# The next expert's rows, transposed one part later, in a mixture-of-experts decoder step

## The chip, the core and the metric

The kernel runs on one core of a Trainium2 chip. The metric is the device time of one execution in microseconds (us). The core has TensorE (PE in the rows, PEld for its weight loads), the vector engine (DVE), the scalar engine (ACT), GpSimd (POOL) and SyncE (SP), which here only issues DMAs. They run apart from one another and meet by semaphores.

## What is computed

One decoder layer for 512 prompt tokens and 32 sample tokens: attention, a short convolution and memory attention, then a mixture of experts, and a last RMSNorm. Each of the 544 tokens goes to 4 of 32 experts. Everything is float32. What matters here is the part for the experts:

```python
h = xb @ w_gate_up[e] + b_gate_up[e]
gate = jnp.minimum(h[:, 0::2], SWIGLU_LIMIT)
up = jnp.clip(h[:, 1::2], -SWIGLU_LIMIT, SWIGLU_LIMIT)
glu = gate * jax.nn.sigmoid(gate * SWIGLU_ALPHA)
return ((up + 1.0) * glu) @ w_down[e] + b_down[e]
```

`xb` are the rows of the tokens that chose expert `e`, with 1024 columns; `w_gate_up[e]` is 1024 x 2048 and `w_down[e]` 1024 x 1024. The results are scaled by the gates and added to the tokens' rows.

## The kernel before

**Stages.** From 0 to some 245 us the kernel does attention, the router and the tables that say which token sits in which slot of which expert. Then come 32 periods, one for each expert. Each expert has 104 slots; a block for overflow stands behind and isn't entered with these inputs.

**Precision.** Each float32 operand is split into a high part (rounded to the fast matmul type, by a cast on ACT) and a low part (the rest, by a subtraction on DVE). A product is then three matmuls: high x high, low x high, high x low (lines 2435, 2436, 2437), each 104 x 512 over 128 rows.

**Parts.** The weights of an expert come as six chunks of 2 MB, each used as two halves. A half is a part: twelve matmuls on TensorE, one cast on ACT (`high_part`, line 1133) and one subtraction on DVE (`low_part`, line 1754). The twelve parts of period `n` are, in TensorE's order: gate-up parts 0 to 5 of expert n, down parts 6 and 7 of expert n, gate-up parts 8 and 9 that already belong to expert n+1, and down parts 10 and 11 of expert n. Between them stand the transposes of the expert's activations: `act_rows`, four transposes each, behind part 4 and behind part 8 (line 2430). Each part ends with one increment of the semaphore `w_used`, which releases buffers for the other engines: after part i of period n it stands at 12n + 3 + i.

**The next expert's rows.** GpSimd gathers them from DRAM two periods ahead (`gather`, line 749; in the loop, from the ninth expert on, behind two small copies of slot tables, lines 740 and 741). TensorE transposes them (`x_rows`, line 2419, eight transposes into two PSUM banks), ACT casts them (`x_high`, line 1164, twice), and DVE subtracts (`x_low`, line 1818, twice). Gate-up part 8 is the first to read them. The first matmul of part 8 also waits for the bias row that ACT copies into its PSUM bank (`bias_seed`, line 1171) and for its weights' low half.

**Order on ACT at the place in question** (i is the part): in step 6 the clamp of the gate (line 1149), `x_high`, the sigmoid (line 1155), the cast of weight part 9 (line 1133), the copy of the first bias row (line 1171). **On DVE** in step 6: the clip (line 1829), `x_low`, the subtraction of weight part 8, and the two products of the SwiGLU (lines 1836 and 1839). The order is written out by hand, in one program per engine. Period 1 alone is written otherwise, by the flag `late`: there the transposes stand behind down part 6, and `x_high` and `x_low` behind the sigmoid and the SwiGLU.

**On GpSimd** in a period: the scatter of the last expert's results into the token table (line 762), two broadcasts of a bias row (line 682), then the wait for `w_used` at 12n + 9 (behind part 6). Behind that wait: in periods 1 to 3 the add of one tile of bias rows (line 814), and in all that still gather, the gather and two more broadcasts. Periods 2 to 6 end with four writes of the slot table (line 733).

Of the kernel before, what the change touches and what calls it, by code (L numbers as in the profile page):

```python
# [55 lines left out]
HALVES = 2 * NCH  # L56
# [56 lines left out]
def build(nc, x_prompt, x_sample, mem_prompt, cache_win_k, cache_win_v, win_kT, mem_kT, cache_mem_v,  # L113
# [4 lines left out]
    with ctx:  # L118
# [13 lines left out]
        def sem(name):  # L132
            if name not in sems:
                sems[name] = ctx.enter_context(nc.semaphore(name))
            return sems[name]
# [34 lines left out]
        def c_(name, rows=P):  # L170
            a, b = _C[name]
            return cst[0:rows, a:b]
# [172 lines left out]
        def row_tile(r):  # L345
            return (memrow[:, r, :], P) if r < 2 else (xrow[0:ROWS[r - 2], r - 2, :], ROWS[r - 2])
# [293 lines left out]
        def _(pool):  # L640
# [6 lines left out]
            for r in range(7):  # L647
                n = row_tile(r)[1]
# [130 lines left out]
            def period(n, k, last=False, table=False, bare=False, overflow=False):  # L779
                old = not (last or table or bare)  # L780
                if old:
                    slots(n + 2, k)
                if not isinstance(n, int) or n > 0:
                    scatter(n, k)
                if not last:
                    if overflow:
                        bias_rows(n + 1, 0)
                    bias_rows(n + 1, 1)
                    pool.wait_ge(sem("w_used"), n * HALVES + 9)
                if isinstance(n, int) and 0 < n < UB:  # L790
                    pool.wait_ge(sem("scattered"), n * 16)
                    add_bias(n + 1)
                if table:
                    table_slots(n + 2, k + 2)
                if old or table:
                    gather(n + 2, k + 2, table)
                if old and not overflow or table:
                    bias_rows(n + 2, 0)
                if old and isinstance(n, int) and 2 <= n < 7:
                    table_rows(4 * (n - 2), 4 * (n - 1))  # L800
# [67 lines left out]
        def _(ac):  # L868
# [3 lines left out]
            for r in range(7):  # L872
                ap, n = row_tile(r)
# [339 lines left out]
            def period(n, k, last=False):  # L1213
                for i in range(10 if last else HALVES):
                    if i == 0 and (not isinstance(n, int) or n > 0):
                        y_rows(n, k, n * HALVES + 2)
                    if i == 2:
                        gate_over(n, 0)
                        gate_sigmoid(n, 0)
                    if i == 6:  # L1220
                        late = isinstance(n, int) and n == 1
                        gate_over(n, 1)
                        if not last and not late:
                            x_high(n + 1)
                        gate_sigmoid(n, 1)
                        if late:
                            x_high(n + 1)
                    if not last or i + 3 < 10:
                        high_part(n, i + 3, last)
                    if isinstance(n, int) and n < UB and (i == 1 or i == 0 == n):  # L1230
                        bias_evict(n + i)
                    if last and i == 5:
                        row_squares(2, 1)
                    if last and i == 6:
                        row_squares(3, 1)
                        row_squares(4, 1)
                    if last and i == 7:
                        act_high(n, 1)
                        row_squares(0, 1)
                        row_squares(1, 1)  # L1240
                    if i == 4:
                        act_high(n, 0)
                    if i == 6 and not last:
                        bias_seed(n + 1, 0)
                    if i == 8 and not last:
                        act_high(n, 1)
                    if i >= 9 and not last:
                        bias_seed(n + 1, i - 8)
# [10 lines left out]
            for c, part in enumerate((2, 3, 2)):  # L1259
                last = nc.scalar.copy(gate3[:, :, c * NE:(c + 1) * NE], rv_all[:, 0:NE, :, part].rearrange("p e j -> p j e"))  # L1260
# [15 lines left out]
            for u in range(2 * UB):  # L1276
                period(u, u)
# [27 lines left out]
        def _(dv):  # L1305
# [296 lines left out]
            for j in range(NTT):  # L1602
                last = v.tensor_scalar(row_i[:, j:j + 1], c_("tokid")[:, j:j + 1], float(NT), None, ALU.add)
# [299 lines left out]
            def period(n, k, last=False, table=False, bare=False):  # L1903
                old = not (last or table or bare)
                for i in range(10 if last else HALVES):
                    if i == 2:
                        clip_up(n, 0)
                    if i == 6:
                        late = isinstance(n, int) and n == 1
                        clip_up(n, 1)  # L1910
                        if not last and not late:
                            x_low(n + 1)
                    if i == (7 if last else 9):
                        act_low(n, 1)
                    if last and i == 7:
                        row_means(3, 1)
                        row_means(4, 1)
                    if i == 10 and old:
                        slot_info(n + 2, k + 2)
                    if not last or i + 2 < 10:  # L1920
                        low_part(n, i + 2, last)
                    if i == 0 and old:
                        hot_slots(n + 2, k)
                    if isinstance(n, int) and n == 0 and i == 4:
                        table_keys()
                    if isinstance(n, int) and n == 0 and i == 8:
                        table_tops()
                    if isinstance(n, int) and n == 1 and i in (1, 4, 7, 10):
                        table_gates(i // 3)
                    if i == 2:  # L1930
                        swiglu(n, 0)
                    if i == 4:
                        act_low(n, 0)
                    if i == 6:
                        swiglu(n, 1)
                        if late:
                            x_low(n + 1)
                    if last and i == 6:
                        row_means(2, 1)
                        row_weights(0, 1)  # L1940
                        row_weights(1, 1)
# [29 lines left out]
        def _(pe):  # L1971
# [366 lines left out]
            for c in range(2):  # L2338
                last = tr(banks[7][0:18, 256 + c * P:256 + (c + 1) * P], ul[:, c, :], ident)
# [156 lines left out]
            def period(n, k, last=False, table=False, bare=False, overflow=False):  # L2496

                early = n if isinstance(n, int) and n < UB else None
                if early == 0:
                    bias_term(0)  # L2500
                if early is not None:
                    pe.wait_ge(sem("gcol_ready"), early + 2)
                    bias_term(early + 1)
                gate_up(n, 0, last, k)
                gate_up(n, 1, last, k)
                gate_up(n, 2, last, k)
                gate_up(n, 3, last, k)
                if early is not None:
                    pe.wait_ge(sem("bias_row"), 2 * early + 4)
                gate_up(n, 4, last, k)  # L2510
                act_rows(n, 0, overflow)
                gate_up(n, 5, last, k)
                late = isinstance(n, int) and n == 1
                if not last and not late:
                    x_rows(n + 1, k + 1)
                wait(pe, "yrow_ready", n * 2)
                down(n, 6, last)
                if late:
                    x_rows(n + 1, k + 1)
                down(n, 7, last, middle=last)  # L2520
                if not last:
                    pe.wait_ge(sem("x_low"), n * 2 + 4)
                    gate_up(n, 8, last, k + 1)
                    act_rows(n, 1)
                    gate_up(n, 9, last, k + 1)
                    if not (table or bare):
                        info(n + 2, k)
                down(n, 8 if last else 10, last)
                down(n, 9 if last else 11, last)
# [3 lines left out]
            for j in range(NTT):  # L2533
                last = mm(banks[6][0:CAP, 416:418], hot[:, 0, j, :], rv_all[:, 0, j, 0:2], start=(j == 0), stop=(j == NTT - 1))
# [4 lines left out]
            for j in range(NTT):  # L2539
                last = mm(banks[6][0:CAP, 416:420], hot[:, 0, j, :], rv_all[:, 0, j, :], start=(j == 0), stop=(j == NTT - 1))  # L2540
# [4 lines left out]
            for q in range(4):  # L2545
                last = mm(banks[q][0:CAP, :], bias_r[:, 0:CAP], bias_r[:, 0:512], start=True, stop=True)
# [67 lines left out]
```

## Time and profile before

| what | value |
|---|---|
| median of 3 runs | 1394.35 us (1400.48, 1394.35, 1393.88) |
| profiled execution | 1399.39 us, of which the span is 1397.5 |
| mean granted clock of TensorE | 0.989 of full speed |
| busy: TensorE, DVE, ACT, GpSimd | 1359.8, 1206.0, 1070.6, 759.1 us |
| moved by DMA | 461.48 MB, 330 GB/s in the mean |

The span runs from the first to the last instruction; the profiled execution's own time is 1.9 us longer. Busy time is the time in which an engine has an instruction in hand; for TensorE the ends of matmuls are modelled and overlap, so the distance between two starts tells more than the duration of one. A timeline row gives the start, the duration, the engine, the line, the operation, what it writes and reads, a count of merged instructions, and in brackets the idle time just before it and what ended that. Where several semaphores are waited for, the one named is the one that the profile found last; a DMA can be the true one. A row by stage gives the stretch, its length, and busy time with the count of instructions for PE, PEld, DVE, ACT and POOL.

### The profile page before, as it was taken

To read this page: it belongs to the slowest core of one execution; us is meant where nothing else is said; L and a number is where in the kernel's file an instruction comes from. 1 tells how busy PE (TensorE), PEld (TensorE's weight loads), DVE (VectorE), ACT (ScalarE), POOL (GpSimd) and SP (SyncE) were. 2 spreads that over 40 slices of the span, in tenths; PEclk is the share of its full clock that TensorE was granted. 3 is DMA by queue.
4 is the path that set the end of the run, shared out by engine and by line. 5 is a ranking of instruction groups with operands and counts; after the bars stand their busy time and mean duration, and the time that the engine had idled before them with its cause. 6 is when DMAs were issued, how large, how long until landed. Compare 5 with 4: busy or idle time off the path is not lost.

```text
span 1397.5 us, 19410 instructions
## 1 busy us (share of the span) xinstructions
PE 1359.8 (97%) x6775; PEld 1000.4 (72%) x6775; DVE 1206.0 (86%) x1098; ACT 1070.6 (77%) x1102; POOL 759.1 (54%) x363
## 2 busy tenths in 40 slices
PE   9999998999997999999999999999999999999995
PEld 6988655667775777777777777777777777777773
DVE  5466555899996999999999999999999999999996
ACT  5354413878885888888888888888888888888884
POOL 2022112386775979656666666566665666665403
PEclk9999999999998999999999999999999999999998
DMA  9522171999997999999999999999999999999984
GB/s 353 196 66 83 75 286 61 367 378 372 388 391 269 363 386 364 366 387 382 381 390 388 369 385 369 382 384 376 383 381 370 383 376 378 391 376 377 383 304 149
DMA packets 52506, 461.48 MB, mean 330 GB/s; under 512 B 11545, under 2 KB 15611, under 8 KB 26825
## 3 DMA queue, kind: packets, MB, share of 16 engines
q1 hardware_dynamic: 40169, 438.59, 80.2%
q0 software_dynamic: 10624, 20.42, 6.5%
q10 hardware_dynamic: 1648, 1.65, 0.4%
q8 instruction: 36, 0.59, 0.2%
q14 instruction: 29, 0.24, 0.0%
HBM read 446.88 MB, written 24.31 MB: 337 GB/s over the span
## 4 chain that ended last, share of the span: by engine, by line
PE 67%; DMA 2%; issue 1%; POOL 1%; DVE 0%; ACT 0%; POOLq 0%; ACTq 0%; DVEq 0%
PE psum L2437 21%; PE psum L2436 21%; PE psum L2435 21%; PE psum L2419 1%; PE psum L2430 1%; DMA area<-hn_tbl,idx_i 1%; POOL small L840 0%; DMA y_tbl<-area,idx_i 0%; POOL brow L682 0%; DVE low L1754 0%; PE psum L2406 0%; DVE ring L1900 0%; POOL out L850 0%; ACT area L1202 0%; ACT ring L1210 0%
## 5 line engine op out<-in xcount | busy, mean ns | idle before, releaser
L1754 DVE TENSOR_TENSOR low<-raw,high 128x2048 fp32r<-128x2048 f32 x384 | 868.2, 2292 | 36.8 <-ACT high L1133 36.7
L1133 ACT CAST high<-raw 128x2048 fp32r<-128x2048 f32 x384 | 727.8, 1912 | 39.0 <-PE psum L2437 35.0
L2435 PE MATMUL psum<-high,area_r 128*104 128x512 f32 x1536 | 610.8, 398 | 3.8 <-DVE area_r L1823 1.5
L2437 PE MATMUL psum<-low,area_r 128*104 128x512 f32 x1536 | 604.7, 394 | 0.0
L2436 PE MATMUL psum<-high,area_r 128*104 128x512 f32 x1536 | 604.3, 393 | 0.0
L2437 PEld LDWEIGHTS psum<-low,area_r 128*104 128x104 f32 x1536 | 258.2, 168 | 96.7
L2435 PEld LDWEIGHTS psum<-high,area_r 128*104 128x104 f32 x1536 | 258.4, 168 | 95.9 <-DVE area_r L1818 2.1
L2436 PEld LDWEIGHTS psum<-high,area_r 128*104 128x104 f32 x1536 | 258.6, 168 | 91.0
L682 POOL PARTITION_BROADCAST brow<-brow x128 | 253.1, 2047 | 27.8 <-issue 15.0
L749 POOL DMA_INDIRECT area<-hn_tbl,idx_i x32 | 173.5, 5423 | 71.7 <-DVE idx_i L1721 42.6
L679 POOL COPY arrived<-cst 1x1 f32 x40 | 84.8, 2121 | 123.0 <-DMA brow<-in_biases 123.0
L762 POOL DMA_INDIRECT y_tbl<-area,idx_i x31 | 110.7, 3571 | 39.1 <-ACT area L1143 27.1
L740 POOL CAST idx_i<-us 104x1 int32 (+1 forms) x22 | 17.8, 807 | 135.9 <-PE psum L2437 135.9
L1159 ACT CAST area_r<-psum 128x416 fp32r<-128x416 f32 x64 | 32.4, 506 | 73.3 <-PE psum L2430 73.3
L659 POOL TENSOR_TENSOR ring<-ring,small 128x512 f32<-128x512 f32 (+2 forms) x18 | 24.2, 1358 | 111.5 <-DVE small L1425 111.5
L1171 ACT COPY psum<-brow 104x512 f32<-104x512 f32 x128 | 75.5, 591 | 0.0
L1149 ACT ACTIVATE area<-psum,cst 104x512 f32<-104x512 f32 x64 | 44.1, 689 | 29.7 <-PE psum L2437 29.7
L733 POOL DMA_INDIRECT slot_tbl<-wr,us x20 | 50.8, 2538 | 5.4 <-issue 5.4
L2196 PE MATMUL psum<-ring,area 128*128 128x512 f32 x112 | 52.4, 601 | 0.0
L1823 DVE TENSOR_TENSOR area_r<-psum,area_r 128x416 fp32r<-128x416 f32 x64 | 37.5, 587 | 15.5 <-ACT area_r L1159 15.4
L1155 ACT ACTIVATE area<-area,cst 104x512 f32<-104x512 f32 x64 | 47.0, 735 | 2.8
L1143 ACT ACTIVATE area<-psum,area 104x512 f32<-104x512 f32 x62 | 39.3, 686 | 12.8 <-PE psum L2437 12.8
(287 smaller groups left out, 1229.5 us busy)
## 6 DMA issues: line engine op xcount, KB each, us to landing
raw<-in_w_gate_up SPq DMA_DIRECT2D x128, 2048.0 KB, 12.2
raw<-in_w_down SPq DMA_DIRECT2D x64, 2048.0 KB, 11.7
ring<-in_w_in SPq DMA_DIRECT2D x7, 1024.0 KB, 16.2
ring<-in_x_prompt SPq DMA_DIRECT2D x8, 512.0 KB, 9.6
ring<-in_w_out SPq DMA_DIRECT2D x7, 512.0 KB, 4.4
ring<-in_w_mem_kv SPq DMA_DIRECT2D x2, 1024.0 KB, 9.4
ring<-in_mem_kT SPq DMA_DIRECT2D x1, 2048.0 KB
ring<-in_cache_mem_v SPq DMA_DIRECT2D x1, 2048.0 KB, 8.4
```

The costliest lines, as they stand in the source:

```text
L679: nc.gpsimd.tensor_copy(arrived[0:1, part:part + 1], seen[:, bass.ds(n, 1), 0])
L682: nc.gpsimd.partition_broadcast(brow[:, cols], brow[0:1, cols], channels=P).then_inc(sem("bias_cast"), 1)
L733: nc.gpsimd.indirect_dma_start(slot_tbl[:, :], bass.IndirectOffsetOnAxis(ap=slot_i[0:n, i:i + 1].bitcast(U32), axis=0), slot_row[0:n, i, : ...
L749: nc.gpsimd.indirect_dma_start(xg[0:CAP, k % 2, :], None, hn_tbl[:, :], bass.IndirectOffsetOnAxis(ap=idx_i[0:CAP, k % UB:k % UB + 1].bitca ...
L762: nc.gpsimd.indirect_dma_start(y_tbl[:, :], bass.IndirectOffsetOnAxis(ap=idx_i[0:CAP, (k - 1) % UB:(k - 1) % UB + 1].bitcast(U32), axis=0) ...
L1133: nc.scalar.copy(high_w(i), raw_w(t)).then_inc(sem("w_high"), 1)
L1171: nc.scalar.copy(banks[q][0:CAP, :], brow[0:CAP, q * 512:(q + 1) * 512]).then_inc(sem("spare_bias_in"), 1)
L1754: v.tensor_tensor(low_w(t), raw_w(t), high_w(i), ALU.subtract).then_inc(sem("w_low"), 1)
L2196: last = mm(bank[0:n, :], zT[:, t, j * P:j * P + n], wo[t][:, half * 512:(half + 1) * 512], start=(t == tiles[0]), stop=(t == tiles[-1]))
L2435: mm(bank, high, wh, start=start, stop=False, skip_group_check=True)
L2436: mm(bank, low, wh, start=False, stop=False, skip_group_check=True)
L2437: return mm(bank, high, wl, start=False, stop=stop, skip_group_check=True)
```

## The change

The flag `late`, so far true in period 1 alone, becomes true in each period from 1 to 30, on all three engines. GpSimd's wait behind which it gathers goes from the end of part 6 to the end of part 7.

```diff
@@ GpSimd, period
-                    pool.wait_ge(sem("w_used"), n * HALVES + 9)
+                    pool.wait_ge(sem("w_used"), n * HALVES + 10)
@@ ACT, period
                     if i == 6:
-                        late = isinstance(n, int) and n == 1
+                        late = not last and (not isinstance(n, int) or n > 0)
                         gate_over(n, 1)
                         if not last and not late:
                             x_high(n + 1)
@@ DVE, period
                     if i == 6:
-                        late = isinstance(n, int) and n == 1
+                        late = not last and (not isinstance(n, int) or n > 0)
                         clip_up(n, 1)
                         if not last and not late:
                             x_low(n + 1)
@@ TensorE, period
                 gate_up(n, 5, last, k)
-                late = isinstance(n, int) and n == 1
+                late = not last and (not isinstance(n, int) or n > 0)
                 if not last and not late:
                     x_rows(n + 1, k + 1)
                 wait(pe, "yrow_ready", n * 2)
```

How the instructions stand then. On TensorE in period 2 (the third expert) the transposes follow gate-up part 5, and down part 6 comes behind them. Before:

```order
L2437 MATMUL psum<-low,area_r 104x512
L2419 MATMUL psum<-cst,area 128x104 [waits act_low,gathered]
L2419 MATMUL psum<-cst,area 128x104 x7
L2435 MATMUL psum<-high,area_r 104x512 [waits w_low,act_low,yrow_ready]
L2436 MATMUL psum<-high,area_r 104x512
L2437 MATMUL psum<-low,area_r 104x512
```

After, at the same transposes, now with down part 6 ahead of them and down part 7 behind:

```order
L2437 MATMUL psum<-low,area_r 104x512
L2419 MATMUL psum<-cst,area 128x104 [waits act_low,gathered]
L2419 MATMUL psum<-cst,area 128x104 x7
L2435 MATMUL psum<-high,area_r 104x512 [waits w_low]
L2436 MATMUL psum<-high,area_r 104x512
```

The twelve matmuls of part 6 changed places with the eight transposes. In both kernels gate-up part 8 begins with a matmul that waits for w_low, spare_bias_in (the bias copy) and x_low.

On ACT in the same period (L1149 is the clamp, L1164 the cast of the transposed rows, L1155 the sigmoid, L1133 the cast of a weight part, L1171 the bias copy), - is before and + after:

```order
 L1133 CAST high<-raw 128x2048 [waits w_used,chunk0]
 L1149 ACTIVATE area<-psum,cst 104x512 [waits w_used]
-L1164 CAST area_r<-psum 128x416 [waits xg_pe] x2
-L1155 ACTIVATE area<-area,cst 104x512 [waits over_ready,glu_ready]
+L1155 ACTIVATE area<-area,cst 104x512 [waits over_ready,glu_ready]
+L1164 CAST area_r<-psum 128x416 [waits xg_pe] x2
 L1133 CAST high<-raw 128x2048 [waits w_used,chunk0]
 L1171 COPY psum<-brow 104x512 [waits glu_made,bias_cast]
```

The casts of the rows moved behind the sigmoid; the weight cast and the bias copy still follow them.

On DVE (L1829 the clip, L1818 the subtraction for the rows, L1754 that of a weight part, L1836 and L1839 the SwiGLU):

```order
 L1829 TENSOR_SCALAR area<-psum 104x512 [waits act_pe,w_used]
-L1818 TENSOR_TENSOR area_r<-psum,area_r 128x416 [waits x_high] x2
-L1754 TENSOR_TENSOR low<-raw,high 128x2048 [waits w_high]
-L1836 SCALAR_TENSOR_TENSOR area<-psum,area 104x512 [waits sig_ready]
-L1839 SCALAR_TENSOR_TENSOR area<-area 104x512 [waits up_ready,glu_made]
+L1754 TENSOR_TENSOR low<-raw,high 128x2048 [waits w_high]
+L1836 SCALAR_TENSOR_TENSOR area<-psum,area 104x512 [waits sig_ready]
+L1839 SCALAR_TENSOR_TENSOR area<-area 104x512 [waits up_ready,glu_made]
+L1818 TENSOR_TENSOR area_r<-psum,area_r 128x416 [waits x_high] x2
 L1754 TENSOR_TENSOR low<-raw,high 128x2048 [waits w_high] x2
```

The subtraction for the rows moved behind one weight part and the SwiGLU. On GpSimd and SP no instruction moves.

## Rows read from the trace of the kernel before

**Rows 1.** The page: busy time of the engines, and the chain that ended last by line.

```profile
PE 1359.8 (97%) x6775; PEld 1000.4 (72%) x6775; DVE 1206.0 (86%) x1098; ACT 1070.6 (77%) x1102; POOL 759.1 (54%) x363
...
PE psum L2437 21%; PE psum L2436 21%; PE psum L2435 21%; PE psum L2419 1%; PE psum L2430 1%; DMA area<-hn_tbl,idx_i 1%; POOL small L840 0%; DMA y_tbl<-area,idx_i 0%; POOL brow L682 0%; DVE low L1754 0%; PE psum L2406 0%; DVE ring L1900 0%; POOL out L850 0%; ACT area L1202 0%; ACT ring L1210 0%
```

**Rows 2.** Busy time by stage; last columns: granted clock, DMA share, GB/s.

```profile
600.00:700.00 100.00, 100.00 (x465) 73.61 (x464) 93.59 (x64) 85.79 (x76) 60.23 (x29) 1.00 1.00 381
```

**Rows 3.** TensorE's timeline, steady state: start us, us, engine, line.

```profile
710.01 0.88 PE L2419 MATMUL psum<-cst,area 104*128 104x104 f32 x8
...
744.66 0.88 PE L2419 MATMUL psum<-cst,area 104*128 104x104 f32 x8
...
750.93 0.39 PE L2435 MATMUL psum<-high,area_r 128*104 128x512 f32 x1
...
753.70 0.52 PE L2430 MATMUL psum<-cst,area 104*128 104x104 f32 x4
```

**Rows 4.** Line 2419, all its instructions: duration min/median/max in ns, first and last start.

```profile
L2419 PE MATMUL psum<-cst,area x256: 250/252/435, 246.1 to 1334.4; 104*128 104x104 f32 x128
```

**Rows 5.** TensorE's timeline around its long wait.

```profile
428.77 1.65 PE L2419 MATMUL psum<-cst,area 104*128 104x104 f32 x8 [9.60 <-DMA area<-hn_tbl,idx_i]
...
439.73 0.52 PE L2430 MATMUL psum<-cst,area 104*128 104x104 f32 x4
```

**Rows 6.** Busy time by stage, the end of the long wait.

```profile
424.00:428.70 4.70, 0.00 (x0) 0.00 (x0) 0.00 (x0) 0.00 (x0) 3.54 (x5) 0.50 0.90 307
```

**Rows 7.** TensorE's timeline in period 1, and one row of period 2.

```profile
314.31 0.88 PE L2419 MATMUL psum<-cst,area 104*128 104x104 f32 x8
...
318.75 0.48 PE L2435 MATMUL psum<-high,area_r 128*104 128x512 f32 x1 [0.78 <-DVE area_r L1818]
...
321.62 0.52 PE L2430 MATMUL psum<-cst,area 104*128 104x104 f32 x4
...
357.24 0.52 PE L2430 MATMUL psum<-cst,area 104*128 104x104 f32 x4
```

**Rows 8.** ACT's timeline in period 1, and its bias copy in steady state.

```profile
314.86 0.92 ACT L1164 CAST area_r<-psum 128x416 fp32r<-128x416 f32 x2 [2.54 <-PE psum L2419]
...
315.66 1.92 ACT L1133 CAST high<-raw 128x2048 fp32r<-128x2048 f32 x1
...
317.47 0.60 ACT L1171 COPY psum<-brow 104x512 f32<-104x512 f32 x1
...
748.66 0.61 ACT L1171 COPY psum<-brow 104x512 f32<-104x512 f32 x1
```

**Rows 9.** Timeline ahead of the experts: an ACT copy that TensorE waits for.

```profile
233.25 0.40 ACT L1012 COPY area<-psum 128x128 f32<-128x128 f32 x2
...
233.70 0.22 PEld L2248 LDWEIGHTS psum<-area,wr 128*32 128x32 f32 x16 [0.92 <-ACT area L1012]
```

**Rows 10.** DVE's timeline: periods 1 and 2, and steady state.

```profile
313.48 0.68 DVE L1829 TENSOR_SCALAR area<-psum 104x512 f32<-104x512 f32 x1
...
317.61 1.08 DVE L1818 TENSOR_TENSOR area_r<-psum,area_r 128x416 fp32r<-128x416 f32 x2
...
349.86 0.68 DVE L1829 TENSOR_SCALAR area<-psum 104x512 f32<-104x512 f32 x1
...
745.34 0.68 DVE L1829 TENSOR_SCALAR area<-psum 104x512 f32<-104x512 f32 x1
```

**Rows 11.** GpSimd's timeline: periods 2 and 3, and the loop.

```profile
363.12 7.38 POOL L749 DMA_INDIRECT area<-hn_tbl,idx_i  x1 [2.20 <-DVE idx_i L1721]
...
407.96 3.94 POOL L814 DMA_INDIRECT y_tbl<-area,row_i  x1 [7.76 <-PE psum L2437]
...
748.51 0.80 POOL L740 CAST idx_i<-us 104x1 int32 x1 [5.73 <-PE psum L2437]
...
761.88 2.47 POOL L679 COPY arrived<-cst 1x1 f32 x1 [5.89 <-DMA brow<-in_biases]
```

**Rows 12.** The chain of waits, the piece before 428.72: start us, us.

```profile
412.20 16.52 DMA area<-hn_tbl,idx_i
```

## The prediction

> **What bounds the kernel now.** I read four views, from the coarse to the fine. The page first: TensorE is busy for 97% of the span, and the chain that ended last runs through matmul lines 2435 to 2437 for 63% of it [rows 1]. Then a table by stage: from 600 to 700 us TensorE is busy for 100.00 of 100 us at granted clock 1.00, with DVE at 93.59 and the DMA share at 1.00 [rows 2]. So three resources are nearly full, and only TensorE has no gap. Third, TensorE's timeline. The transposes of the next expert's rows start at 710.01 and at 744.66 [rows 3]: a period (one step of the loop over experts) is 34.65 us. It stays so: the last of all transposes starts at 1334.4, and the last of the eight at 744.66 starts 0.6 us behind the first, so 17 periods take 589.1 us, 34.65 each [rows 3, 4]. Fourth, the waits around the place that is edited. In steady state TensorE never waits there, so there is no idle time for the edit to win back. It can only win where TensorE does wait: once, 9.60 us before the transposes at 428.77, for a gather [rows 5].
>
> **The steady state: what moves.** Before, the eight transposes stand between gate-up part 5 and down part 6. After, down part 6 goes first. The work is the same: twelve matmuls and eight transposes, in the other order, so the instructions themselves cost nothing. What changes is the distance from the transposes to gate-up part 8, which is the first to use their result. Before, 750.93 - 744.66 = 6.27 us lie between them [rows 3]. After, one down part (twelve matmuls) lies there and not two. A part takes 753.70 - 750.93 = 2.77 us, so 6.27 - 2.77 = 3.50 us remain. The trace has one period in the new order already: period 1, in which the second expert is computed and the rows of the third are transposed. It is my measure for what follows.
>
> **Who must be done within 3.50 us.** The first matmul of gate-up part 8 waits for three things: the split rows (x_low, on DVE), the low half of its weights, and the bias that ACT copies into its bank (line 1171). On ACT the order is: cast of the transposed rows (line 1164, twice), cast of weight part 9 (line 1133), and only then that bias copy. All of it stands behind the wait for the transposes. In the steady period of before, the bias copy starts at 748.66 and takes 0.61 us, ending 1.66 us ahead of the matmul at 750.93 [rows 3, 8]. In period 1 the transposes start at 314.31 [rows 7], and the same three instructions at 314.86, 315.66 and 317.47, the last one for 0.60 us [rows 8]. That ends at 318.07, 3.76 us after the transposes began. An ACT copy that TensorE did wait for ended at 233.25 + 0.40 = 233.65, and TensorE went on at 233.70 [rows 9]. I add these 0.05 us: 3.81 us. The matmul could go at 3.50. So TensorE waits 0.31 us.
>
> In period 1 this wait doesn't show by itself, because DVE was later: x_low started at 317.61 for 1.08 us, and the matmul went at 318.75 [rows 7, 10]. DVE in steady state is earlier. Its chain starts with the clip (line 1829). From there to the end of x_low in the new order period 1 took 317.61 + 1.08 - 313.48 = 5.21 us [rows 10]. The steady period has its clip at 745.34 [rows 10], so x_low ends at 750.55 and is seen 0.06 later (as 318.69 was at 318.75). The matmul would start at 750.93, its weights one step of 0.23 earlier, at 750.70. DVE is thus in time by 0.09 us and is not what ends last; the bias copy, due at 744.66 + 2.77 + 3.81 = 751.24, is.
>
> A wait costs a little more than its length. After the one in period 1 the twelve matmuls took 321.62 - 318.75 = 2.87 us, against 2.77 [rows 3, 7]: 0.10 more. So 0.31 + 0.10 = **0.41 us per period**. The bounds of this term: 0 (should ACT get there sooner) and 1.04, which is what period 1 lost in all (318.75 - 314.31 - 3.50 = 0.94 of wait and 0.10 behind it). I take 0.41, since it is built of the same instructions in the same order.
>
> **Does it come back later?** In the new order ACT starts weight part 9 at 1.35 us behind the transposes (315.66 - 314.31 [rows 7, 8]), later than it could before, and DVE's low part 9 follows. But both have idle time in each period (ACT is busy 85.79 of 100 us, DVE 93.59 [rows 2]). TensorE's own delay gives them as much time again. So I expect one wait per period and no second one, and nothing that gives it back, since TensorE has no other idle time.
>
> **How many periods.** The edit acts in periods 2 to 30 (period 31 has no next expert). Periods 2 and 3 lie ahead of the long wait, which hangs on GpSimd and not on TensorE (below), so what they lose is taken out of that wait. Period 4 holds that wait itself; its matmuls run at the low clock behind it [rows 6], which hides the bias copy. Periods 5 to 30 remain, 26 of them: 26 x 0.41 = **+10.7 us**.
>
> **Period 2 alone.** There DVE is behind: its clip starts at 349.86 [rows 10]. With 5.21 us, x_low ends at 355.07. Gate-up part 8 stands at 357.24 - 2.77 = 354.47 [rows 7], so TensorE loses 355.13 - 354.47 + 0.10 = 0.76 us, and 0.41 in period 3. Both are absorbed.
>
> **The one long wait.** The gather for the sixth expert starts at 412.20 and lands 16.52 us later, at 428.72 [rows 12]. It is late because GpSimd has four table writes, a scatter and the add of a bias row ahead of it, and the last, at 407.96, waits 7.76 us [rows 11]. The row names TensorE, whose release is long past; what can still be open is the landing of that scatter. None of these waits for TensorE's part 6 or 7: the release that the edit moves came long before, and GpSimd's gather at 363.12 was started by DVE's indices [rows 11]. So 428.72 stays. TensorE comes to the transposes later by one part, since it does down part 6 first: 2.77 us of work move out of the time behind the wait into the wait. **Gain 2.8 us**, once. 
>
> **The gathers held one part longer.** In the loop GpSimd waits for the release (5.73 us before 748.51) and, once the gather is issued, waits again, 5.89 us, for the bias row before 761.88 [rows 11]. A start 2.77 us later is taken up by the second wait. Behind the held instruction queue the gather, two broadcasts and the next scatter; only the gather moves. It lands in some 17 us (16.52 above), its rows are read by the transposes 779.31 - 748.51 = 30.8 us after its start, and the reader moves by the same part. Cost 0. Without that cover it would cost at most 2.77 us per period. SP's bias loads follow ACT's bias copies, half a microsecond later, and the 2 MB load behind them moves with them; it has a whole part of lead, so 0.
>
> **Sum.** +10.7 - 2.8 = +7.9 us. The profiled execution took 1399.39 us (span 1397.5 and 1.9 around it), so it would take 1407.3. The median of the runs shown is 1394.35, 5.0 lower; two runs are at 1394 and one at 1400, so I put the difference on the median: **1402.2 us**.
>
> **Rivals.** (1) *No wait for the bias copy.* If ACT's chain or TensorE's own delay leave the copy in time (0.31 us are enough), only the gain is left: 1394.35 - 2.8 = 1391.6, not slower than before. For it: the margin is small, and before had 1.66 us there. Against it: period 1 shows the whole ACT chain in this order. Chance 0.10. (2) *DVE ends last, as in period 1.* It decides once x_low is later than 3.76 us after the transposes; 1.04 us in each of 26 periods is 27.0, so 1394.35 + 27.0 - 2.8 = 1418.6. Against it: DVE's steady clip is followed by 5.21 us, which fits; in period 1 DVE had extra table work ahead. Chance 0.04. (3) *The long wait differs between runs.* The 5 us between the profiled run and the median may be that wait. Then before has less to win, or the clock stays up: 10.7 - 4.7 = +6.0, 1400.4, within 0.5%. I count it as the lower half of my forecast. (4) *The clock falls with each short wait.* The rows speak against it: period 1 has a wait of 0.78 us, and the twelve matmuls behind it took 2.87 us, 0.24 each [rows 7], where a granted clock of 0.50 would have doubled that. Would it fall, each period would lose 1.9 us more: 26 x 1.9 = 49, 1394.35 + 7.9 + 49 = 1451. Chance 0.01. The Trainium skill (TensorE: Matmul & The Clock Gate, section "A second HAM failure mode: psum-queue depth-cycling") says that TensorE's frequent micro-idles between groups of matmuls can make its clock oscillate between half and full rate. By that rule this change, which puts a bubble into each period, would be a bad one; the trace does not agree so far.
>
> **How the numbers follow.** My forecast, the bias copy waited for in each period, has 0.83; the rest is left for causes that I don't see. Within 0.5% of 1394.35 is 1387.4 to 1401.3; a measurement of this kernel can hardly tell less from no change. The forecast's centre is only 0.9 above that edge. With 0.32 to 0.50 us per period (8.3 to 13.0) and a gain of 4.7 to 0 its own range is 1398 to 1407, some seven tenths of it above the edge. Slower: 0.83 x 0.73 + 0.05 = 0.66. Within: 0.83 x 0.27 + 0.08 = 0.30. Faster: 0.04. The range for 8 in 10 reaches one step towards rival 1 and takes in the slower kind of run: 1396.5 to 1408.5.
>
> **What would show it.** In the changed kernel's timeline: transposes between down parts 6 and 7; on TensorE, at the first matmul of gate-up part 8, a gap of some 0.3 us with ACT line 1171 as its releaser; periods of 35.06 us and not 34.65; transposes at about 428.8 with a wait of 5 to 6 us. Periods of 34.65 would make rival 1 right, 35.7 and DVE line 1818 as releaser rival 2. I am wrong in kind if another wait appears, or if a period differs from 34.65 for another reason.

## The result

The changed kernel takes 1401.89 us (median of 7 runs, 1400.33 to 1404.02), the kernel before 1394.68 in its 7 runs of the same comparison. The ratio is 1.0045, 95% interval 1.0025 to 1.0065. So it is slower by 0.45% by the ratio, and the medians lie 7.2 us apart; 1402.2 was forecast. The profiled execution took 1400.33 us with a span of 1398.5, only 1 us above the one of before, because that was itself a long one (1399.39).

Busy time by stage after (PE, PEld, DVE, ACT, POOL, then granted clock, DMA share, GB/s), the stretch of [rows 2]:

```profile
600.00:700.00 100.00, 99.28 (x455) 72.25 (x454) 92.60 (x64) 86.42 (x76) 56.91 (x30) 1.00 0.99 376
```

TensorE is no longer busy for all of the 100 us: 0.7 us are idle, at the same clock. TensorE's timeline of one steady period shows where, answering to [rows 3]:

```profile
739.88 0.79 PE L2419 MATMUL psum<-cst,area 104*128 104x104 f32 x7
...
775.02 0.88 PE L2419 MATMUL psum<-cst,area 104*128 104x104 f32 x8
...
778.29 0.40 PE L2437 MATMUL psum<-low,area_r 128*104 128x512 f32 x1
...
778.93 0.47 PE L2435 MATMUL psum<-high,area_r 128*104 128x512 f32 x1 [0.24 <-ACT psum L1171]
...
781.80 0.52 PE L2430 MATMUL psum<-cst,area 104*128 104x104 f32 x4
```

The period is 35.14 us where it was 34.65. (The first row says x7 because the view shown ended inside the group of eight.) The first matmul of gate-up part 8 goes at 778.93; one step of 0.23 us behind the last one would be 778.52. It waits 0.41 us, and ACT's bias copy is named. (The 0.24 in brackets is less, since the end of the matmul before is modelled.) Part 8 then takes 781.80 - 778.93 = 2.87 us and not 2.77. ACT and DVE in the same period, answering to [rows 8, 10]:

```profile
775.58 0.91 ACT L1164 CAST area_r<-psum 128x416 fp32r<-128x416 f32 x2 [1.62 <-PE psum L2419]
776.38 1.93 ACT L1133 CAST high<-raw 128x2048 fp32r<-128x2048 f32 x1
778.20 0.61 ACT L1171 COPY psum<-brow 104x512 f32<-104x512 f32 x1
```

```profile
772.92 0.68 DVE L1829 TENSOR_SCALAR area<-psum 104x512 f32<-104x512 f32 x1
...
777.05 1.08 DVE L1818 TENSOR_TENSOR area_r<-psum,area_r 128x416 fp32r<-128x416 f32 x2
```

The bias copy starts 3.18 us behind the transposes and ends at 778.81; x_low ended at 778.13, so DVE was in time. And ACT stands idle for 1.62 us right before these casts. At the place of the long wait [rows 5] the transposes for the sixth expert now start without one:

```profile
421.77 0.88 PE L2419 MATMUL psum<-cst,area 104*128 104x104 f32 x8
...
425.64 0.45 PE L2435 MATMUL psum<-high,area_r 128*104 128x512 f32 x1 [0.21 <-issue]
```

### The profile page after: what moved, and what is told of

The parts are those of the page before. It is cut to its first block, busy times and chain, and to the rows that moved or that the text cites. A ratio compares the mean times of both kernels' runs of the same rounds, so it can differ in the third digit from the quotient of the medians.

```text
span 1398.5 us, 19410 instructions
## 1 busy us (share of the span) xinstructions
PE 1365.6 (98%) x6775; PEld 999.0 (71%) x6775; DVE 1209.1 (86%) x1098; ACT 1070.8 (77%) x1102; POOL 638.0 (46%) x363
## 4 chain that ended last, share of the span: by engine, by line
PE 80%; DVE 6%; ACT 5%; issue 4%; DMA 2%; POOL 1%; SPq 0%; ACTq 0%; POOLq 0%; DVEq 0%
PE psum L2435 21%; PE psum L2436 21%; PE psum L2437 21%; PE psum L2196 4%; DVE low L1754 3%; ACT high L1133 3%; PE psum L2033 2%; PE psum L2035 2%; PE psum L2034 2%; PE psum L2430 1%; DMA y_tbl<-area,row_i 1%; DMA ring<-in_x_prompt 1%; PE psum L2419 1%; ACT psum L1171 1%; PE psum L1977 1%
## 5 line engine op out<-in xcount | busy, mean ns | idle before, releaser
L1754 DVE TENSOR_TENSOR low<-raw,high 128x2048 fp32r<-128x2048 f32 x384 | 870.2, 2292 | 46.9 <-ACT high L1133 45.9
L1133 ACT CAST high<-raw 128x2048 fp32r<-128x2048 f32 x384 | 725.2, 1914 | 34.4 <-PE psum L2437 31.8
L682 POOL PARTITION_BROADCAST brow<-brow x128 | 232.5, 1885 | 43.9 <-DMA brow<-in_biases 37.5
L740 POOL CAST idx_i<-us 104x1 int32 (+1 forms) x22 | 39.8, 1808 | 253.3 <-PE psum L2437 253.3
L749 POOL DMA_INDIRECT area<-hn_tbl,idx_i x32 | 98.0, 3063 | 59.4 <-DVE idx_i L1721 34.7
L679 POOL COPY arrived<-cst 1x1 f32 x40 | 58.2, 1456 | 121.8 <-DMA brow<-in_biases 121.8
L762 POOL DMA_INDIRECT y_tbl<-area,idx_i x31 | 84.9, 2739 | 37.9 <-ACT area L1143 27.5
L1171 ACT COPY psum<-brow 104x512 f32<-104x512 f32 x128 | 75.6, 591 | 1.2 <-PE psum L2546 1.2
L1164 ACT CAST area_r<-psum 128x416 fp32r<-128x416 f32 x64 | 29.3, 509 | 50.6 <-PE psum L2419 50.6
L1149 ACT ACTIVATE area<-psum,cst 104x512 f32<-104x512 f32 x64 | 44.2, 690 | 29.7 <-PE psum L2437 29.7
L1159 ACT CAST area_r<-psum 128x416 fp32r<-128x416 f32 x64 | 32.5, 508 | 38.2 <-PE psum L2430 38.2
L733 POOL DMA_INDIRECT slot_tbl<-wr,us x20 | 58.9, 2946 | 5.4 <-issue 5.4
L1155 ACT ACTIVATE area<-area,cst 104x512 f32<-104x512 f32 x64 | 46.5, 726 | 5.1
L1823 DVE TENSOR_TENSOR area_r<-psum,area_r 128x416 fp32r<-128x416 f32 x64 | 37.8, 590 | 13.5 <-ACT area_r L1159 13.4
```

The source lines that it names most:

```text
L679: nc.gpsimd.tensor_copy(arrived[0:1, part:part + 1], seen[:, bass.ds(n, 1), 0])
L682: nc.gpsimd.partition_broadcast(brow[:, cols], brow[0:1, cols], channels=P).then_inc(sem("bias_cast"), 1)
L733: nc.gpsimd.indirect_dma_start(slot_tbl[:, :], bass.IndirectOffsetOnAxis(ap=slot_i[0:n, i:i + 1].bitcast(U32), axis=0), slot_row[0:n, i, : ...
L749: nc.gpsimd.indirect_dma_start(xg[0:CAP, k % 2, :], None, hn_tbl[:, :], bass.IndirectOffsetOnAxis(ap=idx_i[0:CAP, k % UB:k % UB + 1].bitca ...
L762: nc.gpsimd.indirect_dma_start(y_tbl[:, :], bass.IndirectOffsetOnAxis(ap=idx_i[0:CAP, (k - 1) % UB:(k - 1) % UB + 1].bitcast(U32), axis=0) ...
L1133: nc.scalar.copy(high_w(i), raw_w(t)).then_inc(sem("w_high"), 1)
```

## The experiments

All times are medians, with the ratio to the kernel before in the same comparison.

**The kernel before, once more (before_again).** No edit.

> The kernel before, once more, for a second trace of its early periods. Theory: the long wait of TensorE before the transposes of the sixth expert's rows (9.60 us in the first trace) differs between executions, and is shorter in one near the median: at 1394 us it should be 3 to 6 us, the periods from the ninth expert on stay at 34.65 us. Rival: the wait is as long as before and the 5 us between the profiled execution and the median lie elsewhere.

One run, 1392.33 us. TensorE's timeline and the busy time by stage around the long wait:

```profile
421.12 1.65 PE L2419 MATMUL psum<-cst,area 104*128 104x104 f32 x8 [3.41 <-DMA area<-hn_tbl,idx_i]
...
432.88 0.52 PE L2430 MATMUL psum<-cst,area 104*128 104x104 f32 x4
```

```profile
419.00:421.00 2.00, 0.00 (x0) 0.00 (x0) 0.00 (x0) 0.00 (x0) 1.39 (x3) 0.77 0.97 365
421.00:423.00 2.00, 1.88 (x10) 1.75 (x11) 0.35 (x1) 0.70 (x2) 1.69 (x2) 0.50 0.99 418
...
427.00:429.00 2.00, 2.00 (x11) 1.43 (x10) 2.00 (x2) 1.42 (x1) 2.00 (x2) 1.00 0.67 225
```

Here the wait is 3.41 us and not 9.60, and that is 6.2 of the 6.9 us by which this trace's span (1390.6) is shorter than the first one's (1397.5). So the 5 us between the profiled execution and the median were mostly this wait, as far as two traces can say. Even so the granted clock fell to 0.50, and stayed there for some 6 us: the way to the next four-part transpose took 432.88 - 421.12 = 11.76 us against the 9.04 of a steady period, 2.7 us more. The short wait cost 3.4 + 2.7 us. The steady period stays 34.65.

**The bias copy first (seed_first).** The changed kernel, with

```diff
                         if late:
+                            bias_seed(n + 1, 0)
                             x_high(n + 1)
@@
-                    if i == 6 and not last:
+                    if i == 6 and not last and not late:
                         bias_seed(n + 1, 0)
```

> The changed kernel with one instruction of ACT moved: the copy of the next expert's first bias row (line 1171) stands right behind the sigmoid, ahead of the casts of the transposed rows, in the 1.6 us in which ACT waits for TensorE there. Theory (the bias copy is what part 8 waits for): the gap on TensorE goes, periods return from 35.14 to 34.65 or 34.7 us, 26 x 0.48 = 12.5 us less than the changed kernel: about 1389.5 us. Rival (DVE's x_low is as late, the copy only the last to be named): periods stay above 34.9 with line 1818 as releaser, 1396 us or more.

1388.29 us, ratio 0.9963 (0.9951 to 0.9975). The copy now stands in ACT's idle time, ahead of its casts, and the last of all transposes (here line 2420, the file being one line longer) comes at 1326.8 where the changed kernel had 1337.8:

```profile
769.78 0.73 ACT L1155 ACTIVATE area<-area,cst 104x512 f32<-104x512 f32 x1
770.41 0.58 ACT L1171 COPY psum<-brow 104x512 f32<-104x512 f32 x1
772.12 0.92 ACT L1164 CAST area_r<-psum 128x416 fp32r<-128x416 f32 x2 [1.14 <-PE psum L2420]
772.92 5.54 ACT L1133 CAST high<-raw 128x2048 fp32r<-128x2048 f32 x3
```

```profile
L2420 PE MATMUL psum<-cst,area x256: 250/252/281, 247.8 to 1326.8; 104*128 104x104 f32 x128
```

The periods are 34.66 us. One instruction moved takes the loss away, and what is left of the change is a gain. The theory holds, and so does DVE's margin: from period 3 on part 8 follows without a gap in every period, with DVE's x_low where it was in the changed kernel (its end 3.10 us behind the transposes, 774.67 - 771.57).

**The hold alone (hold_only).** The kernel before, with `n * HALVES + 10` in GpSimd's wait.

> The kernel before with nothing but GpSimd's wait moved from the end of part 6 to the end of part 7. Theory: the wait for the bias row behind the gather takes the delay up, no effect: within 1 us of before, periods of 34.65 us. Rival (the shorter GpSimd instructions of the changed kernel's trace come from the later gather, and they shorten the early chain): 2 to 5 us faster than before and a wait of under 3 us before the sixth expert's transposes.

1393.20 us, ratio 0.9999 (0.9989 to 1.0009): nothing, and periods of 34.65. GpSimd's timeline in the loop, answering to [rows 11]:

```profile
746.46 4.09 POOL L740 CAST idx_i<-us 104x1 int32 x1 [7.48 <-PE psum L2437]
...
751.54 9.25 POOL L749 DMA_INDIRECT area<-hn_tbl,idx_i  x1 [0.88 <-POOL area L741]
760.81 0.18 POOL L679 COPY arrived<-cst 1x1 f32 x1
```

The same gather takes 9.25 us here where it took 5.68 before, so the second wait, for the bias row, is gone and GpSimd goes on at once. It gets to the copy ahead of its broadcasts (line 679) some 4 us later in the period than before: 760.81 is 21.0 us behind the transposes (739.84), where 761.88 was 17.2 behind them (744.66). The wait for the release then takes that up: it is 4.5 to 7.7 us in the loop, in turn. So the delay is covered, though not by the second wait alone, as the prediction had it. The hold alone doesn't shorten GpSimd's instructions in the loop.

The reverse, the changed kernel with the wait put back to part 6, was not tried: without the hold the gather for the expert after next may land before TensorE's wait for the next one's, and both count on the same semaphore. That is what the hold is there for, by the program; no run shows it.

**The new order early only (early_only).** In all three engines of the changed kernel:

```diff
-late = not last and (not isinstance(n, int) or n > 0)
+late = isinstance(n, int) and 1 <= n <= 4
```

> The changed kernel with the new order in periods 1 to 4 alone; from period 5 on the transposes stand where they stood before. Theory (all of the gain lies at the long wait for the sixth expert's gather, all of the loss in the periods behind it): no 0.48 us per period, the gain of some 5 us stays: about 1389.5 us, periods of 34.65. Rival (the gain is only the 2.8 us of one part): 1391.9 us. Rival (no gain at all in runs near the median): 1394.7 us.

1389.07 us, ratio 0.9972 (0.9959 to 0.9986): the median is 4.7 us below before, nearer to 5 than to 2.8. The interval reaches from 2.0 to 5.7 us and holds both, so the times rule out only the rival of no gain, and the trace has to decide. Its span of 1386.7 is 3.9 below before_again's. It has no wait for the sixth expert's gather, and the clock stays up:

```profile
422.12 0.88 PE L2419 MATMUL psum<-cst,area 104*128 104x104 f32 x8
...
425.99 0.45 PE L2435 MATMUL psum<-high,area_r 128*104 128x512 f32 x1 [0.20 <-issue]
```

**The new order in the loop only (loop_only).** `late` in period 1 and from period 5 on.

> The changed kernel with the new order in period 1 and from period 5 on; periods 2, 3 and 4 stand as before, so the long wait should be there as before. Theory (26 periods lose 0.48 us each, and the early gain of 5 us is not had): 12.5 us slower than the kernel before, 1406 us against 1393.7, periods of 35.14, a wait of 3 us or more before the sixth expert's transposes. Rival (loss and gain are not separate, since the faster early periods of the changed kernel come from something in the loop's order): as the changed kernel, 1401 us.

1402.33 us, ratio 1.0078 (1.0050 to 1.0107), 9.0 us above before; its six runs spread from 1400.15 to 1411.71. The interval, 7.0 to 14.9 us, holds the 12.5 us that were expected, but also the 7.6 of the rival, and the median is nearer to that. The trace decides: it is as the theory has it, with periods of 35.17, a wait of 3.58 us at the sixth expert, and a span of 1402.6 against 1390.6 for the kernel before's second trace, 12.0 us. (That execution took 1404.46, 2.1 us above its median.)

```profile
420.29 1.65 PE L2419 MATMUL psum<-cst,area 104*128 104x104 f32 x8 [3.58 <-DMA area<-hn_tbl,idx_i]
...
747.21 0.47 PE L2435 MATMUL psum<-high,area_r 128*104 128x512 f32 x1 [0.25 <-ACT psum L1171]
```

**The bias copy later (seed_late).** The changed kernel, from period 5 on with

```diff
-                    if i == 6 and not last:
+                    if not last and i == (7 if not isinstance(n, int) or n >= 5 else 6):
                         bias_seed(n + 1, 0)
```

> The changed kernel with ACT's copy of the first bias row one weight cast further back (behind the cast of part 10) in the periods from 5 on: the suspected cost made larger by one cast, 1.8 us. Theory (the copy's place alone sets the gap): the gap grows from 0.41 to 2.2 us, periods of 36.95 us, 26 x 1.81 = 47 us more than the changed kernel, 1449 us, with line 1171 as releaser and the granted clock still 1.00. Rival (short waits in each period make the clock fall): a granted clock well under 1.00 in the loop and 1490 us or more. Rival (something else ends last there): less than 20 us more than the changed kernel.

1462.09 us, ratio 1.0495 (1.0472 to 1.0519). 1449 was expected, so both the theory and the rival about the clock have a share. TensorE's timeline in two periods, and the busy time by stage around the two waits:

```profile
613.77 0.47 PE L2435 MATMUL psum<-high,area_r 128*104 128x512 f32 x1 [2.04 <-DVE low L1754]
...
616.63 0.52 PE L2430 MATMUL psum<-cst,area 104*128 104x104 f32 x4
```

```profile
650.71 0.64 PE L2435 MATMUL psum<-high,area_r 128*104 128x512 f32 x1 [2.04 <-DVE low L1754]
...
655.13 0.52 PE L2430 MATMUL psum<-cst,area 104*128 104x104 f32 x4
```

```profile
613.00:617.00 4.00, 3.23 (x17) 2.45 (x18) 2.89 (x2) 2.48 (x3) 3.12 (x3) 1.00 0.96 336
650.00:654.00 4.00, 3.29 (x8) 2.34 (x9) 2.82 (x2) 2.40 (x3) 3.12 (x3) 0.61 0.98 375
```

From the ninth expert on most periods are 36.93 us, 1.8 above the changed kernel's, as one cast of delay says. But eight of the 26 measure 38.5: the same 2.04 us of wait, and part 8 takes 655.13 - 650.71 = 4.42 us and not 2.86, at a granted clock of 0.61 in the mean. Eight times 1.55 is 12.4 us, nearly all of the 13 us by which the time is above the expected one. The releaser named is not line 1171, as was expected, but DVE's line 1754. Yet the bias copy started at 613.04 and took 0.60 us, so it ended 0.13 us ahead of the matmul, as in the changed kernel (0.12). The subtraction named, from 611.40 on, is one that follows x_low, so it is of weight part 9 and not what part 8 needs: in the changed kernel the same one (from 778.35 on) had not ended when part 8 started at 778.93.

**Both useful steps (early_seed).** The new order in periods 1 to 4, with the bias copy first in these.

> The two useful steps together: the new order in periods 1 to 4 alone, and in these the bias copy right behind the sigmoid. Theory: the waits of 0.2 us (0.44 us in all) of periods 3 and 4 go too, and that of period 2 stays, since DVE is late there: 1 us less than with the new order in periods 1 to 4 and the old place of the copy, so 1388 us, 0.4% below the kernel before. Rival (periods ahead of the gather only wait longer for it): no difference from that kernel, 1389 us.

1388.39 us, ratio 0.9961 (0.9947 to 0.9975); early_only had 0.9972. The difference is within the intervals; the waits of 0.2 us are gone from periods 3 and 4 in its trace. It is level with seed_first, and these two are the fastest.

**Which early period makes the gain (p4_only, p23_only).** `late` in periods 1 and 4, and in periods 1, 2 and 3.

> The changed kernel with the new order in periods 1 and 4 alone. Period 4 holds the wait for the sixth expert's gather, 3.4 us in the traces near the median. Theory (the gain is one part of 2.8 us done inside that wait, and with it the clock that no longer falls): the wait shrinks to some 0.6 us, no stretch at a granted clock of 0.50 behind it, 4 to 5 us below the kernel before, about 1389 us. Rival (the gain comes from periods 2 and 3 reaching the wait later): less than 2.8 us below before, 1391 us or more.

> The changed kernel with the new order in periods 1, 2 and 3 alone. Theory: TensorE loses about 1.2 us in periods 2 and 3, reaches the wait for the sixth expert's gather so much later, waits some 2.2 us there and finds the clock at half rate behind it: no gain and no loss, 1393.4 us, within 1 us of the kernel before. Rival (periods 2 and 3 make the gain): 1390 us or less.

p4_only takes 1389.86 us, ratio 0.9972 (0.9956 to 0.9989), as expected, though the interval also reaches down to 1.5 us of gain. The trace is clearer: 0.73 us of wait are left, and the clock stays up. p23_only takes 1391.28, ratio 0.9979 (0.9964 to 0.9993). That is a gain of 2.8 us (interval 1.0 to 5.0) where none was expected. TensorE's timelines, p4_only and then p23_only, with the stage behind the wait of the first:

```profile
422.22 0.94 PE L2419 MATMUL psum<-cst,area 104*128 104x104 f32 x8 [0.73 <-DMA area<-hn_tbl,idx_i]
```

```profile
422.00:424.00 2.00, 1.78 (x13) 1.54 (x14) 1.97 (x5) 1.17 (x3) 1.70 (x2) 1.00 0.95 402
```

```profile
420.56 0.93 PE L2419 MATMUL psum<-cst,area 104*128 104x104 f32 x8 [0.74 <-DMA area<-hn_tbl,idx_i]
```

In p23_only, too, only 0.74 us were waited, not 2.2, and the clock stayed up. TensorE came some 1.2 us later, and GpSimd issued the gather at 406.70 where before_again has 407.69. So two ways lead to a wait short enough to keep the clock, and the gain isn't period 4's alone. That it is smaller than early_only's has a counterpart in the trace: the four periods from the sixth expert's transposes to the tenth's take 142.7 us, where four at the 35.17 that the kernel before has there would take 140.7. Two waits of 0.19 us in them name DVE's line 1754; what makes the rest isn't known.

**The changed kernel, once more (after_again).** No edit.

> The changed kernel once more, on the same chip as these two and beside runs of the kernel before, for a second trace of it. Theory: periods of 35.1 us from the ninth expert on, no wait before the sixth expert's transposes or one of under 1 us, 7 to 8 us slower than the kernel before, 1401 us against 1393.5. Rival (the early gain of its first trace was chance): a wait of 3 us or more, and 10 us or more slower.

1402.35 us, ratio 1.0054 (1.0036 to 1.0072), no wait at the sixth expert again, periods of 35.1. So it was no chance that the wait and the fall of the clock are gone. But the two traces of the changed kernel are not alike ahead of that place. TensorE's transposes and GpSimd's gather for the sixth expert in this trace, and then the gather in the first one:

```profile
424.72 0.88 PE L2419 MATMUL psum<-cst,area 104*128 104x104 f32 x8
```

```profile
409.53 2.00 POOL L749 DMA_INDIRECT area<-hn_tbl,idx_i  x1 [0.30 <-issue]
```

```profile
398.57 3.97 POOL L749 DMA_INDIRECT area<-hn_tbl,idx_i  x1 [0.30 <-issue]
```

In the first trace the gather is issued 11 us earlier and lands 14.9 us later, at 413.5, long before TensorE comes (421.77). Here it lands 13.4 us after its start, at 422.9, still 1.8 us ahead of TensorE, which comes 3 us later than in the first trace. Why the two differ isn't known.

## Why the prediction was right

**The loss.** Forecast: 26 gaps of 0.41 us, 10.7 in all, from ACT's bias copy. From the sixth expert's transposes to the last ones the changed kernel takes 1337.8 - 421.8 and before_again 1327.5 - 421.1, with the eight transposes' own 0.6 us in both: 9.6 us more. The clock gave back 2.7 of them, so the gaps cost 12.3. There are 26 of them in this stretch too, but they are those of periods 4 to 29, 0.47 each; the one of period 30 lies behind the last transposes. So 27 periods pay and not 26, 12.7 us in all: since the clock didn't fall, period 4 isn't hidden behind it, as I had it, but has its gap (at 425.64). The mechanism was right, the term was 2.0 us too small, 1.6 by the size of a gap and 0.4 by the count. What was short in the size is the last step from ACT's end to TensorE's start. I took 0.05 us from [rows 9]; in this place it is 778.93 - 778.81 = 0.12, and the copy started 3.18 and not 3.16 us behind the transposes. The wait is then 0.41 and not 0.31, and with 0.10 behind it 0.51; why a period grows by 0.04 less is open. seed_first shows that the copy's place alone makes the gap, seed_late that it grows with the copy's lateness.

**The gain.** Forecast: 2.8 us, with bounds of 0 and 4.7. Measured by early_only: 4.7 by the medians, with an interval of 2.0 to 5.7, so the size rests on the traces. The step that failed is the choice of 2.8 by the 9.60 us of one profiled execution. In the runs near the median the wait is some 3.4 us, and with one part done inside it and 1.2 us lost ahead of it nothing is left to wait for, so the clock doesn't fall (early_only and after_again: the gather lands 2.0 and 1.8 us before TensorE comes). What I had as rival 3 is what happens. The gain is then 2.7 from the clock and 1.9 from the wait itself, ahead of the sixth expert's transposes (421.77 - 246.19 - 2.77 = 172.8 against 421.12 - 246.46 = 174.7). The 2.7 are the same in both traces of the changed kernel. The 1.9 are not: in early_only they are 1.7, and in after_again only 0.3. That the 4.6 lie at my upper bound of 4.7 is chance, since that was added up from 2.8 and 1.9, measured behind a longer wait.

**The sum.** 12.7 - 4.6 = 8.1 us, by the traces, of which the spans show 7.9 (1398.5 against 1390.6), against 7.2 by the medians and 7.9 forecast. The loss was 2.0 too small and the gain 1.8, and that they cancel, so that the centre was met so closely, is luck. In after_again, with 0.3 for 1.9 and its first transposes 1.1 us later, the span is 11.3 us above before_again's; its execution was 1.3 us above its median.

**The rest.** DVE was in time: x_low ended at 778.13 and was not waited for (rival 2 falls, and seed_first needs the same margin). The hold cost nothing. The clock didn't fall with gaps of 0.4 us, so rival 4 is wrong at this size; at 2.04 us it begins to be right, in eight periods. The Trainium skill's rule on micro-idles (TensorE: Matmul & The Clock Gate, "A second HAM failure mode: psum-queue depth-cycling") thus agrees with eight of the 26 waits in seed_late and with none in the changed kernel. In period 2 DVE's x_low was forecast to be waited for by 0.66 us; from start to start it is 0.92 in after_again and 0.37 in the first trace of the changed kernel (0.75 and 0.20 in brackets). I had also held that the early chain on GpSimd doesn't move, and so that the gather lands at 428.72 in any case. It does move, also between executions of one kernel: it is issued at 412.20 and 407.69 in the two traces of the kernel before, and at 398.57 and 409.53 in those of the changed one. The 428.72 was the latest landing of the four. Why, and why GpSimd's instructions differ in length between the kernels, stays open.

## What to carry to other kernels

When a step is moved nearer to its reader, follow each engine that stands behind the same wait, also for work that has nothing to do with the step: here a bias copy of 0.6 us behind a weight cast was the last to be ready, and moving it into idle time turned +0.5% into -0.4%. A place in the same trace that is already in the new order is the best measure there is. And a wait that varies between executions should be taken from more than one of them, near the median, with the clock that falls behind it counted in.

## What the hardware showed

- A wait of TensorE of 3.41 us was followed by some 6 us at a granted clock of 0.50, for 2.7 us; the one of 9.60 cost 1.9. Waits of 0.73 to 0.79 us left it at 1.00. Of 26 waits of 2.04 us eight brought it down, at 1.55 us each, and eighteen didn't.
- The matmuls behind a wait of 0.4 us are slower as well: part 8 takes 2.87 us behind one and 2.77 without. At 2.04 us with the clock still at 1.00 it is 2.86.
- The same gather instruction on GpSimd took 5.68 us in the loop of the kernel before, 2.26 us in that of the changed one and 9.25 us in that of hold_only, within 0.03 us in each. It falls at another place beside the other engines' work in each; that this is the cause is not shown. None of it reached TensorE in the loop.
